# One stick-breaking attention layer on one core: steps in pairs, and changed ends

## The reference, cut to what matters

```
def stick_breaking_attention(q, k, v):
    """A[t,s] = beta[t,s] * prod_{s<j<t} (1-beta[t,j]), s<t only."""
...
        z = jnp.einsum('bthd,bshd->bhts', q[:, t0:kend], k[:, :kend]).astype(jnp.float32) * scale
        log_beta = jax.nn.log_sigmoid(z)
        log_rem = jnp.where(mask, jax.nn.log_sigmoid(-z), 0.0)
        after = lax.cumsum(log_rem, axis=3, reverse=True) - log_rem
        w = jnp.where(mask, jnp.exp(log_beta + after), 0.0)
...
    proj = jnp.einsum('bsd,de->bse', h, w_in)
    q, k, v, g = jnp.split(proj, 4, axis=-1)
...
    return jnp.einsum('bse,ed->bsd', o * jax.nn.silu(g), w_out)
```

## Time and profile before

| | |
|---|---|
| median of 3 runs | 1672.78 us (1670.83 to 1673.14) |
| the profiled execution | 1671.81 us, its span 1670.1 us |
| mean granted TensorE clock | 0.998 |
| TensorE busy | 1647.5 us, 8600 matmuls |
| VectorE busy | 1351.8 us |
| ScalarE busy | 906.1 us |
| GpSimd busy | 224.3 us |

### The profile page before, as it was taken

The page is one execution under the profiler, slowest core; times in us unless marked ns, Lnnn a source line. Parts: engine busy times, 40 slices in busy tenths (PEclk is TensorE's granted clock), DMA queues, the critical chain, the costliest instruction groups (busy, mean ns, idle before and its releaser), DMA issues.

```text
span 1670.1 us, 23300 instructions
## 1 busy us (share of the span) xinstructions
PE 1647.5 (99%) x8600; PEld 1377.3 (82%) x8600; DVE 1351.8 (81%) x1885; ACT 906.1 (54%) x1779; POOL 224.3 (13%) x212
## 2 busy tenths in 40 slices
PE   8999999999999999999999999999999999999998
PEld 7888878888888888888888888888888888778786
DVE  5535379889898988989888998898988888956765
ACT  6635256655665565656565555566565656651122
POOL 0020012110111011101110211011201110008400
PEclk9999999999999999999999999999999999999999
DMA  9858534252524243334334351425243335398632
GB/s 316 266 166 285 175 119 147 81 152 67 155 77 132 80 136 106 97 101 127 113 90 121 95 145 58 145 77 145 76 126 107 114 95 163 124 357 269 228 140 107
DMA packets 164225, 237.09 MB, mean 142 GB/s; under 512 B 49936, under 2 KB 91920, under 8 KB 164112
## 3 DMA queue, kind: packets, MB, share of 16 engines
q1 hardware_dynamic: 94624, 160.03, 30.8%
q10 hardware_dynamic: 69488, 75.58, 15.2%
HBM read 155.78 MB, written 79.76 MB: 141 GB/s over the span
## 4 chain that ended last, share of the span: by engine, by line
PE 90%; DVE 3%; DMA 3%; issue 1%; ACT 1%; SPq 1%; POOL 0%; ACTq 0%; DVEq 0%
PE proj_ps L740 29%; PE turn_ps L767 14%; PE z_ps L758 7%; PE z_ps L757 7%; PE o_ps L782 7%; PE o_ps L781 7%; PE proj_ps L695 5%; PE o_ps L695 3%; PE turn_ps L695 3%; PE turn_ps L811 3%; PE proj_ps L811 2%; PE z_ps L811 2%; DMA wo_raw<-in_w_out 1%; DMA qk_lo_cols<-made_lo 1%; DVE o_part_hi L1187 1%
## 5 line engine op out<-in xcount | busy, mean ns | idle before, releaser
L933 ACT ACTIVATE u<-z_ps 128x512 f32<-128x512 f32 (+3 forms) x640 | 341.8, 534 | 410.3 <-PE z_ps L758 407.8
L1158 DVE TENSOR_TENSOR_SCAN u<-u,u 128x512 f32<-128x512 f32 x384 | 490.9, 1279 | 0.0
L1163 DVE TENSOR_TENSOR r_turned_lo<-turn_ps,r_turned_hi 128x512 fp32r<-128x512 f32 (+3 forms) x640 | 381.1, 596 | 105.6 <-ACT r_turned_hi L939 100.6
L939 ACT ACTIVATE r_turned_hi<-turn_ps 128x512 fp32r<-128x512 f32 (+3 forms) x640 | 340.1, 531 | 59.0 <-issue 46.2
L767 PE MATMUL turn_ps<-ident,u 128*128 128x128 f32 x2176 | 343.1, 273 | 0.0
L671 POOL TENSOR_SCALAR w_raw<-w_raw,a_norm_col 128x128 f32<-128x128 f32 x192 | 166.8, 889 | 1208.4 <-DMA w_raw<-in_w_qkg 1208.4
L740 PE MATMUL proj_ps<-hT_hi,w_hi 128*128 128x512 f32 x768 | 320.2, 417 | 0.0
L740 PE MATMUL proj_ps<-hT_lo,w_hi 128*128 128x512 f32 x768 | 319.9, 417 | 0.0
L740 PE MATMUL proj_ps<-hT_hi,w_lo 128*128 128x512 f32 x768 | 319.8, 416 | 0.0
L767 PEld LDWEIGHTS turn_ps<-ident,u 128*128 128x128 f32 x2176 | 267.8, 140 | 59.2 <-DVE u L1158 0.3
L781 PE MATMUL o_ps<-r_turned_hi,dv_head 128*128 128x512 f32 (+3 forms) x640 | 230.6, 360 | 5.1 <-ACT o_stage L945 2.0
(11 more groups left out here) (122 smaller groups left out, 1646.3 us busy)
## 6 DMA issues: line engine op xcount, KB each, us to landing
qk_hi_cols<-made_hi ACTq DMA_DIRECT2D x64, 256.0 KB, 2.5
qk_lo_cols<-made_lo ACTq DMA_DIRECT2D x64, 256.0 KB, 3.1
x_T<-in_xT SPq DMA_DIRECT2D x30, 512.0 KB, 6.1
w_raw<-in_w_qkg SPq DMA_DIRECT2D x24, 512.0 KB, 3.5
x_rows<-in_x SPq DMA_DIRECT2D x16, 512.0 KB, 4.7
v_rows<-v_stage ACTq DMA_DIRECT2D x32, 256.0 KB
v_here<-v_rows SPq DMA_DIRECT2D x64, 128.0 KB, 2.8
v_next<-v_rows SPq DMA_DIRECT2D x64, 128.0 KB, 3.2
```

The costliest lines, as they stand in the source:

```text
L933: nc.scalar.activation(u_t[(m // CB) % RU][STEPS[m][3]][:, 0:w], z_ps[m % RZ][:, 0:w], ACT.Sigmoid, scale=-Z_SCALE).then_inc(s_u, 1)
L939: nc.scalar.activation(rt_hi[m % RT][:, 0:w], t_ps[m % RT][:, 0:w], ACT.Copy).then_inc(s_hi, 1)
L1158: nc.vector.tensor_tensor_scan(u, u, other, start, ALU.mult, op).then_inc(s_r, 1)
L1163: nc.vector.tensor_tensor(rt_lo[m % RT][:, 0:w], t_ps[m % RT][:, 0:w], as_f32(rt_hi[m % RT][:, 0:w]), ALU.subtract).then_inc(s_lo, 1)
```

## The change

The steps of the attention are issued in pairs. TensorE's list for a pair n, n + 1 is: the turns of n + 2 and n + 3, three fill matmuls, the scores of n + 10, the rest of the fill, the weighings of n and n + 1, the scores of n + 11. ScalarE's list is paired to match: the two high parts come first, then one sigmoid, the projection's work, the other sigmoid, and then weights and pieces. VectorE's list for the steps stays. The banks are given out anew: one for scores (`RZ` = 1) and four for turned blocks (`RT` = 4), which also get a fourth pair of tiles; the room comes from the second staging tile for o (`RO` = 1).

At the ends, five groups of the projection come first instead of four. The output weights are loaded in two halves: the first four row blocks once chunk 0 of `hT` is no longer read, the last four as before. The high part is made six steps after the load's place. The first pieces come 4, 3 and 2 steps later. `HI_W` and `LO_W` come two steps later relative to the load, and `PAIR_LO` one. In the output stage VectorE makes the two additions of each group that GpSimd made, and `gated_low` moves behind the first block of its turn.

```
-AT_RT = BASE + 56 * KB
+AT_RT = [(BASE + a * KB, BASE + b * KB) for a, b in ((56, 58), (60, 62), (64, 66), (82, 92))]
-LEAD_SCORES = 9
+LEAD_SCORES = 10
-RU, RZ, RT, RO, RP = 3, 2, 3, 2, 2
+RU, RZ, RT, RO, RP = 3, 1, 4, 1, 2
+PAIR = 2
+FILL_FIRST = 3
-BEFORE = 4
+BEFORE = 5
-FILL_NUM, FILL_DEN = 677, 200
+FILL_NUM, FILL_DEN = 6669, 2000
-HI_W = {n + 5: t for n, t in LOAD_W.items()}
-LO_W = {n + 7: t for n, t in LOAD_W.items()}
+HI_W = {n + 7: t for n, t in LOAD_W.items()}
+LO_W = {n + 9: t for n, t in LOAD_W.items()}
-WO_FROM = DONE[GROUP_OF["g", KT - 1, 1]] + 1
-WO_AT = {WO_FROM + k: k for k in range(KT)}
+WO_FROM = [DONE[GROUP_OF["g", KT - 1, c]] + 1 for c in range(2)]
+WO_AT = {WO_FROM[k // (KT // 2)] + k % (KT // 2): k for k in range(KT)}
+WO_HIGH_AT = {n + 6: k for n, k in WO_AT.items()}
-PAIR_LO = each_head((-10, -7, -3, 4))
+PAIR_LO = each_head((-9, -6, -2, 5))
-PIECE_STEP = [SHORT_FROM + 4, SHORT_FROM + 8, SHORT_FROM + 12, LAST_K_FROM + 4] + [REST_FROM + at for at in (6, 7, 8, 10)]
+PIECE_STEP = [SHORT_FROM + 8, SHORT_FROM + 11, SHORT_FROM + 14, LAST_K_FROM + 4] + [REST_FROM + at for at in (6, 7, 8, 10)]
...
@@ GpSimd
-                for t in range(2, TG):
-                    pool.wait_ge(s_in[t % RG], 48 * (t // RG + 1))
-                    nc.gpsimd.tensor_tensor(oa[t % RG][:], oa[t % RG][:], ob[t % RG][:], ALU.add).then_inc(s_sum, 1)
...
-                    nc.gpsimd.tensor_tensor(blocks, blocks, start_v, ALU.add).then_inc(s_start, 1)
@@ TensorE
-                for n in range(-LEAD_SCORES, NS):
-                    if inside(n + LEAD_SCORES):
-                        scores(n + LEAD_SCORES)
-                    if inside(n + LEAD_TURN):
-                        turn(n + LEAD_TURN)
-                    project(filled(n - 1), filled(n))
-                    put_out(out_filled(n - 1), out_filled(n))
-                    if inside(n):
-                        weigh(n)
+                for n in range(-LEAD_SCORES, NS, PAIR):
+                    for m in range(n, n + PAIR):
+                        if inside(m + LEAD_TURN):
+                            turn(m + LEAD_TURN)
+                    begin, end = filled(n - 1), filled(n + PAIR - 1)
+                    middle = min(begin + FILL_FIRST, end)
+                    project(begin, middle)
+                    if inside(n + LEAD_SCORES):
+                        scores(n + LEAD_SCORES)
+                    project(middle, end)
+                    put_out(out_filled(n - 1), out_filled(n + PAIR - 1))
+                    for m in range(n, n + PAIR):
+                        if inside(m):
+                            weigh(m)
+                    if inside(n + 1 + LEAD_SCORES):
+                        scores(n + 1 + LEAD_SCORES)
@@ ScalarE
+                    for m in pair:
+                        if inside(m + LEAD_TURN):
+                            hi(m + LEAD_TURN)
                     if inside(n + LEAD_SCORES):
                         stick(n + LEAD_SCORES)
                     if ended is not None:
                         store_o(ended)
...
+                    for m in pair:
+                        for g in GROUPS_DONE.get(m, []):
+                            made_high(g)
+                    if inside(n + 1 + LEAD_SCORES):
+                        stick(n + 1 + LEAD_SCORES)
+                    for m in pair:
+                        if m in HI_W:
+                            weight_hi(HI_W[m])
...
+                        if m in WO_HIGH_AT:
+                            out_weight_high(WO_HIGH_AT[m])
@@ VectorE
+                def group_start(t):
+                    dve.wait_ge(s_in[t % RG], 48 * (t // RG + 1))
+                    nc.vector.tensor_tensor(oa[t % RG][:], oa[t % RG][:], ob[t % RG][:], ALU.add).then_inc(s_sum, 1)
...
+                    nc.vector.tensor_tensor(blocks, blocks, start_v, ALU.add).then_inc(s_start, 1)
...
                     if t + 1 < TG:
+                        group_start(t + 1)
                         gated(t + 1)
-                        gated_low(t + 1)
                     for n in range(GB * (t - 1), GB * t):
...
                         norm_block(n)
+                        if n % GB == 0 and t + 1 < TG:
+                            gated_low(t + 1)
```

More of the change, by code:

```diff
@@ L294, in all_stages @@
         u_t = [[place(nc, f"u{n}_{r}", [P, CH], F32, AT_U + 2 * KB * (CB * n + r)) for r in range(CB)] for n in range(RU)]
-        rt_hi = [place(nc, f"r_turned_hi{n}", [P, CH], F32R, AT_RT + 4 * KB * n) for n in range(RT)]
-        rt_lo = [place(nc, f"r_turned_lo{n}", [P, CH], F32R, AT_RT + 4 * KB * n + 2 * KB) for n in range(RT)]
+        rt_hi = [place(nc, f"r_turned_hi{n}", [P, CH], F32R, at[0]) for n, at in enumerate(AT_RT)]
+        rt_lo = [place(nc, f"r_turned_lo{n}", [P, CH], F32R, at[1]) for n, at in enumerate(AT_RT)]
         o_st = [place(nc, f"o_stage{n}", [P, CH], F32, AT_OST + 2 * KB * n) for n in range(RO)]
@@ L324, in all_stages @@
         p_ps = [pb(f"proj_ps{n}") for n in range(RP)]
-        row_ps = z_ps + t_ps[:2]
-        v_ps = p_ps + [t_ps[2], o_ps]
-        y_ps = [p_ps, z_ps, t_ps[:2], [t_ps[2], o_ps]]
+        row_ps = t_ps
+        v_ps = p_ps + [z_ps[0], o_ps]
+        y_ps = [p_ps, z_ps + t_ps[3:], t_ps[:2], [t_ps[2], o_ps]]
         s_ident = sem("ident_ready")
@@ L608, in _ @@
                         k = WO_AT[n]
-                        if k == 0:
-                            sp.wait_ge(s_p, GROUP_OF["g", KT - 1, 1] + 1)
+                        if k % (KT // 2) == 0:
+                            sp.wait_ge(s_p, GROUP_OF["g", KT - 1, k // (KT // 2)] + 1)
                         rows = slice(k * P, (k + 1) * P)
@@ L616, in _ @@
                         sp.wait_ge(s_gst, stores_through(GROUP_OF["g", LAST_G - 1, NC - 1]))
-                        for par in range(2):
-                            sp.wait_ge(s_oout[par], 32 * 2 * LAST_G * NC // 2)
+                        for par in range(RO):
+                            sp.wait_ge(s_oout[par], 32 * 2 * LAST_G * NC // RO)
                         load_group(0, slice(0, LAST_G), s_in[0])
@@ L1043, in _ @@
                     v_stored(act, v)
-                for n in range(-LEAD_SCORES, LAST_PIECE_STEP + 1):
+                for n in range(-LEAD_SCORES, LAST_PIECE_STEP + 1, PAIR):
+                    pair = range(n, n + PAIR)
                     ended = chunk_end(n - 1) if inside(n - 1) else None
```

37 lines of the change are left out of this document (15 added, 22 removed).

## The result

The changed kernel takes 1676.62 us (median, 1675.83 to 1679.72) against 1670.83 (1669.07 to 1673.14) for the kernel before on the same chip: ratio 1.0038, 95% interval 1.0026 to 1.0049. The forecast was 1654.4, range 1648 to 1667. The profiled execution of the changed kernel took 1679.72, its span 1678.0.

A forecast was written before the change was run, and what follows sets the result against it. TensorE's own stream plus its losses was taken as the bound. Terms of -10.2 - 1.1 - 1.2 - 3.9 - 3.5 + 0.5 + 1.0 = -18.4 took 1671.8 to 1653.4; 1.0 for the median gave 1654.4 us, range 1648 to 1667.

The forecast's parts named there:

- Lags: Attention steps: longer HI_W and LO_W lags outlast ScalarE's 1.76 us wait, removing two r_turned_lo waits; -1.1 us, bound 0.
- Pairs: Attention steps: joint turns make 640 runs of transposes 320, each saving 0.032 us; -10.2 us, bounds nothing and 14.
- the cost of a run: Attention steps: some eight matmuls behind a run of transposes go slow; priced at 0.032 us a run.
- The argument from the lone transpose: One transpose alone costs as much as a step's four, so the run counts, not its length; supports the 10.2 us.
- The score bank: Attention scores: one bank makes scores wait for ScalarE's sigmoid, mostly hidden; +1.0 us for new waits, between 0 and 4.
- The rival that this bank decides: Attention scores: late ScalarE holds TensorE at the single bank; near 1701 us at 0.15 a pair, 1679 at 0.08; chance 0.09.
- Pieces: First output group: later pieces find the gate load there, but crowd steps 609 to 619; -1.2 us, between -2.7 and +1.5.
- output weights: Last attention steps: loading in halves removes ScalarE's 1.58 us wait, TensorE's idle time and half clock; -3.9 us, bound 0.
- one staging tile: Last chunk of o: its copy must wait for the previous chunk's store to land; +0.5 us, between 0 and +2.7.
- Adds on VectorE: Output stage: VectorE takes GpSimd's additions, so four waits on x_again go; -3.5 us, between -3.5 and +1.
- Five groups first and the fill rate: Before the first score and in the fill: five groups taken at 0, between -1.4 and +1.5; 3.3345 fill at nothing.

The follow-up runs named there:

- pairs_only: The changed kernel's paired steps, banks and tiles with the ends and weight lags of the kernel before: 1692.8 us, ratio 1.0127 to the kernel before.
- w_lo_later: The changed kernel with VectorE's low part of the projection weights 12 steps behind the load instead of 9: 1662.6 us, ratio 0.9950 to the kernel before.
- pool_adds: w_lo_later with the output stage's additions back on GpSimd and gated_low back right behind gated: 1670.5 us, ratio 0.9991 to the kernel before.
- ends_only: The kernel before with only the changed ends, steps single, old fill rate 3.385 kept: 1671.0 us, ratio 1.0002 to the kernel before.
- pairs_lo_later: pairs_only with VectorE's low part of the weights 12 steps behind the load instead of 7: 1674.4 us, ratio 1.0019 to the kernel before.

## Why the prediction was wrong, by its own steps

**The step that failed is "Lags"** ("Longer lags for HI_W and LO_W (two steps, near 4 us) outlast the 1.76 us", -1.1, bound 0). I looked at the two steps that `HI_W` moves against the load. I did not look at the distance that matters to VectorE, from `weight_hi` to `weight_lo`. It is two steps in both kernels, but in the paired list the copy stands up to a pair later in ScalarE's order, and VectorE's list is not paired. The longer lags themselves did not make the loss: pairs_only keeps the old ones and loses 22 us. The term took the waits on r_turned_lo for something that could only shrink (bound 0), and no other term asks what pairing ScalarE's list does to VectorE. Measured: waits on r_turned_lo of 12.4 + 13 x 0.16 against 1.8 + 3 x 0.16, +12.2 instead of -1.1; w_lo_later gets 14.0 back, some of it from the lower clock behind one of the waits. I had asked of each edit what is queued behind a waiting instruction, but only of those that the diff made wait for a new thing, and no wait in VectorE's list is new.

**Pairs** (-10.2). Right in sign for TensorE's small losses, and too large. The small losses in the middle were 17.8 us before, 13.8 in the changed kernel and 11.5 to 12.7 with its stalls mended: for 640 steps a gain of 6 to 7.5. I kept the cost of a run at 0.032. It is 0.033 before (17.8 for 541 steps) and 0.042 to 0.047 for a pair's run, which has twice the matmuls behind it, and two scores. The argument from the lone transpose (it is the run that counts, not its length) took in the cost that each score has by itself. The Trainium skill, "TensorE: Matmul & The Clock Gate", Back-to-back issue gap and LDWEIGHTS, has no such charge; these traces show one.

**The score bank** (+1.0, between 0 and 4). TensorE's waits at the scores went from 1.2 in 1 place to 4.3 in 6, +3.9 with the 0.16 of each: the upper bound. I had listed weight copies, start additions and out-weight copies ahead of the sigmoid. One of the six waits is of that kind (1.2 us at 1464.04, behind two out-weight copies). Three (1.9 us) are `made_high`, standing for the landing of the store before it, which I hadn't listed; the one at 218.92 stands behind a table load of ScalarE (ACT_TABLE_LOAD, 1.28 us), which the kernel before has too. The rival that this bank decides was wrong all the same: 4.3 us in all, and 2.8 to 7.1 in the paired runs. The Trainium skill, "Perfetto Trace Analysis", Optimizing Tensor Performance, wants groups rotated through banks; the runs agree in sign: TensorE waits 4.3 us at the scores with one bank and 1.2 with two. No run changes the bank alone.

**Pieces, output weights, one staging tile** (-1.2 - 3.9 + 0.5 = -4.6). The stretch of 1400 to 1560 gave -1.2. The waits that I named did go: VectorE's at the first piece for the gate load, ScalarE's 1.58 for the last out-weight, the half clock near the last step. No wait shows on the store of o, so its +0.5 is 0. In their place came the early half's own costs: its copies ahead of a sigmoid and of the copy of o (1.66 us on o_stage at 1457.8), and its 4 MB ahead of a gate store. The term of the pieces had a crowd in it at half its gain; that of the output weights had none.

**Adds on VectorE** (-3.5): -3.1 in the trace of the changed kernel, 6.9 by pool_adds. The gate takes 2.29 us throughout, as forecast, though pool_adds shows that this is not where the gain lies. **Five groups first and the fill rate** (0): right in the kernel as it was changed; ends_only shows that the fill rate is not free to choose, since it orders SyncE's queue near step 616.

**The sum.** The ends were forecast at -1.1 - 1.2 - 3.9 - 3.5 = -9.7 and by themselves give -8.0. The rest, pairs with their bank and tile, was forecast at -8.7 and gives 0 with the lists in order, and +14 more as the lists stand: -8.0 + 0 + 14.0 = +6.0, where 5.8 was measured. That it comes out so well is partly luck, since the parts don't simply add: the 0 holds with the changed ends, and with the old ones the mended pairs cost 3.3 (pairs_lo_later). The forecast of 1654.4 was also worked out from a median of 1672.8 for the kernel before (three runs), which was 1670.8 by seven: the terms are off by 24.2 us, and the forecast, with that, by 22.2. None of the rivals was this one. The score bank's rival was priced at 1679, near the measured time, but its 0.08 us in every pair is not what the trace shows: TensorE waits at the scores in six places, and in 13 others, 0.3 to 2.0 us each, for VectorE.

## What to carry to other kernels

When one engine's list is reordered, go through every other engine's list for what it takes from the moved instructions. Count how far behind its maker each use stands in the order in which the two engines really pass their lists, and not in step numbers. Then hold the wait that follows against the distance from the work behind it to its use: here that was some 3 us, waits of up to 2.3 us cost nothing, and waits of up to 4.0 with a 1.2 us operation behind them cost 14 us in all. A part that is moved out of the way of one stall should be asked what it shares a queue with where it lands. And a change made of many parts can hide one bad number behind a net figure: here one constant was worth 14 us, more than the whole of the pairs.

## What the runs showed of the hardware that I had not expected

- TensorE's small losses have places: 3 to 7 ns at each of the next matmuls behind a run of transposes, and 9 to 11 ns between the two matmuls of a full score, also where 13 or more matmuls lie between it and the transposes. An extra run with three matmuls behind it cost 0.010 us; per run, scores included, a step lost 0.033 and a pair 0.042 to 0.047.
- The length of an idle time does not tell whether TensorE's clock falls. At 1057.95 it was 1.68 us and the starts behind it were 0.42 apart. At 1343.00 it was longer and the starts stayed at 0.23 (timeline of the changed kernel):

```profile
1343.00 0.44 PE L776 MATMUL o_ps<-r_turned_hi,dv_head 128*128 128x384 f32 x1 [2.00 <-DVE r_turned_lo L1172]
...
1343.46 0.40 PE L752 MATMUL z_ps<-k_parts,q_parts 128*128 128x512 f32 x1
1343.69 0.39 PE L753 MATMUL z_ps<-k_parts,q_swapped 128*128 128x512 f32 x1
```

- Beside GpSimd's additions (pool_adds) VectorE's operations on 128x1 with two inputs grow from 0.16 us to means of 0.43 to 0.76 and up to 4.53, more in proportion than its large ones. Its RECIPROCAL and TENSOR_SCALAR on 128x1 stay at 0.15 to 0.16.
- A 256 KB gate store lands in 2.6 to 2.8 us (median over a kernel), and in 8.2 and 8.5 when it is issued some 2 us behind 4 MB of output weights and four loads of q.
